# Two prompt tiles of a decoder step share the weight units of their first feed-forward input, and the second tile's x loads behind the first unit

## The reference, cut to what matters

```python
def swiglu_ffn(x, w_in, w_out):
    g, u = jnp.split(x @ w_in, 2, axis=-1)
    return (jax.nn.silu(g) * u) @ w_out
...
    x = x + 0.5 * swiglu_ffn(rmsnorm(x, norm_gains[layer, 0]), ffn_w_in[layer, 0], ffn_w_out[layer, 0])
    h = rmsnorm(x, norm_gains[layer, 1])
    ... GLA in layer 0, windowed attention on shared K/V in layer 1 ...
    x = x + y
    x = x + 0.5 * swiglu_ffn(rmsnorm(x, norm_gains[layer, 2]), ffn_w_in[layer, 1], ffn_w_out[layer, 1])
```

## Time and profile before

| | us |
|---|---|
| median of three runs | 2317.02 |
| lowest and highest | 2314.41, 2321.76 |
| the profiled execution | 2332.64 |
| its span on the slowest core (core 1), first to last instruction | 2331.1 |
| span of its fastest core (core 7) | 2302.8 |
| median span of cores 0 to 3, of cores 4 to 7 | 2321.7, 2309.2 |
| PE busy on core 1 | 2290.8 (98%) |

### The profile page before, as it was taken

How to read it: one execution, slowest core, us unless ns; L and a number is a source line. 1 busy time by engine, 2 the same in 40 slices (tenths; PEclk the granted TensorE clock), 3 DMA queues, 4 the chain that set the end, 5 groups by cost and what they waited for, 6 DMA issues and landing times.

```text
span 2331.1 us, 40261 instructions; the slowest of 8 cores (2302.8 to 2331.1 us)
## 1 busy us (share of the span) xinstructions
PE 2290.8 (98%) x13759; PEld 1080.0 (46%) x13759; DVE 1209.4 (52%) x2094; ACT 1142.2 (49%) x2131; POOL 319.6 (14%) x599
## 2 busy tenths in 40 slices
PE   7999999999999989999999999999999999999999
PEld 3444544544444444445444445445444444444444
DVE  4435664566435566357533445645664355735742
ACT  4434745554543465444552256456455335644551
POOL 2111111111111111110111111111111111011110
PEclk9899999999999999999999999999999999999999
DMA  9998898878988999797999899888899999598793
GB/s 176 149 172 151 153 169 139 136 128 156 164 150 139 182 157 171 137 155 148 167 168 174 151 172 155 146 143 146 155 162 166 159 159 164 102 157 145 148 173 87
DMA packets 101464, 357.08 MB, mean 153 GB/s; under 512 B 12400, under 2 KB 17552, under 8 KB 101136
## 3 DMA queue, kind: packets, MB, share of 16 engines
q0 software_dynamic: 84144, 326.25, 84.5%
q1 hardware_dynamic: 16832, 27.21, 3.7%
q10 hardware_dynamic: 288, 1.05, 0.2%
HBM read 663.17 MB, written 15.40 MB: 291 GB/s over the span
## 4 chain that ended last, share of the span: by engine, by line
PE 95%; DMA 2%; issue 1%; ACT 1%; DVE 1%; POOL 0%; DVEq 0%; SPq 0%; ACTq 0%; POOLq 0%
PE pst L634 91%; PE pst L844 1%; DMA ring<-wfo 1%; DMA ring<-wfi 1%; DMA ring<-ck 1%; PE pst L1461 1%; DMA x<-xp 0%; PE pst L1483 0%; PE pst L1523 0%; PE pst L1096 0%; PE pst L1097 0%; PE pst L1079 0%; ACT h L639 0%; DVE h L650 0%; ACT pb L639 0%
## 5 line engine op out<-in xcount | busy, mean ns | idle before, releaser
L634 PE MATMUL pst<-h,ring 128*128 128x512 bf16 x6144 | 1390.7, 383 | 11.0 <-DMA ring<-wfi 4.3
L634 PEld LDWEIGHTS pst<-h,ring 128*128 128x128 bf16 x6144 | 595.9, 98 | 734.1 <-issue 81.9
L634 PE MATMUL pst<-r,ring 128*128 128x512 bf16 x3136 | 713.0, 382 | 0.8 <-DVE x L650 0.8
L639 ACT ACTIVATE pb<-pb 128x512 f32<-128x512 f32 x856 | 534.7, 630 | 74.8 <-DVE pb L928 13.8
L639 ACT ACTIVATE pb<-pst 128x512 f32<-128x512 f32 (+1 forms) x472 | 278.3, 596 | 506.9 <-PE pst L634 496.5
L647 DVE TENSOR_TENSOR pb<-pb,pst 128x512 f32<-128x512 f32 x368 | 251.7, 686 | 487.2 <-ACT pb L639 484.5
L634 PEld LDWEIGHTS pst<-r,ring 128*128 128x128 bf16 x3136 | 303.8, 98 | 363.1 <-issue 30.0
L530 POOL DMA_DIRECT2D ring<-wfi x336 | 177.8, 531 | 1066.6 <-PE pst L634 852.4
L639 ACT ACTIVATE h<-x 128x512 bf16<-128x512 f32 x188 | 116.8, 627 | 366.4 <-DVE x L650 274.5
L647 DVE TENSOR_TENSOR r<-pb,pst 128x512 bf16<-128x512 f32 x336 | 230.0, 687 | 47.0 <-DVE pb L647 40.1
L650 DVE SCALAR_TENSOR_TENSOR x<-pst,x 128x512 f32<-128x512 f32 x128 | 88.2, 689 | 196.0 <-PE pst L634 193.9
(11 more groups left out here) (159 smaller groups left out, 1006.2 us busy)
## 6 DMA issues: line engine op xcount, KB each, us to landing
ring<-wfi POOLq DMA_DIRECT2D x336, 512.0 KB, 9.5
ring<-wfo POOLq DMA_DIRECT2D x128, 672.0 KB, 8.6
ring<-wgl POOLq DMA_DIRECT2D x64, 512.0 KB, 10.4
y_p<-x SPq DMA_DIRECT2D x32, 256.0 KB, 6.6
x<-xp SPq DMA_DIRECT2D x14, 512.0 KB, 7.8
ring<-wqd POOLq DMA_DIRECT2D x12, 512.0 KB, 12.8
ring<-wod POOLq DMA_DIRECT2D x16, 384.0 KB, 9.4
ring<-wkv POOLq DMA_DIRECT2D x8, 512.0 KB, 7.6
```

The costliest lines, as they stand in the source:

```text
L634: ins = e.matmul(out, lhsT=l, rhs=r, start=(start and i == 0), stop=(stop and i == last), skip_group_check=skip)
L639: return O(ACT, lambda e: e.activation(out=out, in_=in_, func=func, scale=scale, bias=bias), reads, writes, c_act(n))
```

## The change

For t1's first feed-forward input no units are made: `units[(1, "fi0", j)]` is t0's unit. t1 thus reads `ring0`, and those 21 units have three users (t0, ts, t1). The loads of `ring1` begin with t1's `fo0` units, the first four of which wait for t0's `fi0` units 8, 10, 12 and 14. t1's x quarters wait for units 0, 0, 1 and 1 instead of 3, 5, 7 and 9; in the order of building, unit 3 comes behind all four of them. t1 has rank -15 (ahead of the other prompt tile) until its first norm has been applied, and `LEAD` is 21 units instead of 24. Lines behind L463 lie 3 to 7 further down in the changed file (L634 is L641, L844 is L851).

```diff
--- before.py
+++ after.py
@@ -460,7 +460,10 @@
         def ffn_units(f):
             for j in range(NF):
-                add_unit("fi%d" % f, j, wfi[f * NF + j], 2048)
+                if (t, f) == (1, 0):
+                    units[(1, "fi0", j)] = units[(0, "fi0", j)]
+                else:
+                    add_unit("fi%d" % f, j, wfi[f * NF + j], 2048, 0 if t + f else 3)
             for m in range(8):
                 add_unit("fo%d" % f, m, wfo[f * 8 + m], 2688)
                 if (t, f) == (3, 3) and m % 2 == 0:
@@ -491,13 +494,13 @@
-    LEAD = 24 * 2048
+    LEAD = 21 * 2048
     NWS = 8
     first = {(0, "fi0", 0): [("x", "b0", 3)], (0, "fi0", 1): [("x", "b0", 7)]}
     for k in range(4):
-        first[(1, "fi0", k)] = [units[(0, "fi0", 12 + 2 * k)].key]
+        first[(1, "fo0", k)] = [units[(0, "fi0", (8, 10, 12, 14)[k])].key]
     for t in (2, 3):
         for k in range(1, 6):
             first[(t, "fi0", k)] = [("x", "b%d" % (t % 2), 7)]
@@ -517,6 +520,8 @@
             live = [x for x in live if x not in over] + [(lo, hi, u)] + [(a, lo, o) for a, b, o in over if a < lo] \
                 + [(hi, b, o) for a, b, o in over if b > hi]
             u.ap = ring[:, lo:hi]
+            if u.uid == (0, "fi0", 3):
+                yield need(lambda: ("x", "b1", 7) in S.lastw)
             if u.uid in first:
                 yield need(lambda: all(k in S.lastw for k in first[u.uid]) and (u.uid[0] < 2 or ("xl", u.uid[0]) in done))
             dst = u.ap
@@ -562,6 +567,8 @@
         T.nm, T.i, T.t, T.n = "t%d" % t, i, t, 512
         T.rank = (lambda i=i: 10 if i else 0 if prog[0] - prog[1] <= LEAD else 20)
         T.u, T.slot = t, i
+        if t == 1:
+            T.rank = lambda: 10 if ("h", "t1", 1, 7) in done else -15
         T.b = "b%d" % i
         T.x, T.h, T.pool = xb[i], hb[i], Share(pool, i)
         T.R = rb[i]
@@ -668,7 +675,7 @@
             if T.n == 32:
                 yield need(lambda: "CF" in S.lastw)
             if T.t == 1:
-                after = units[(0, "fi0", 3 + 2 * q)]
+                after = units[(0, "fi0", (0, 0, 1, 1)[q])]
                 yield need(lambda: after.ready)
             w = len(ms) * T.n
             src = xp[T.t] if T.n == 512 else xs
```

## The result

The changed kernel is **slower by 0.6%**: 2334.62 us median of seven runs, against 2317.42 us for the kernel before beside it on the same chip, ratio 1.006 with an interval of 1.0049 to 1.0072 (the medians differ by 17.2 us, the ratio, which leaves disturbed runs out, says 13.9). A second measurement on another occasion gave 1.0064 (1.0049 to 1.0079). The prediction was 2313 us, "same" the likeliest; the measured time is also outside its range (2300 to 2327). The start went as rival C said; to that came a base of comparison that was too high, and a second loss behind the start.

The account below looks back on a forecast made before the run. PE was taken as the bound, through its idle time and slow matmuls. 2 us gained at the start, 2 at t0's attention and 0 elsewhere took the median from 2317.0 to 2313 us; 8-in-10 range 2300 to 2327.

Parts of the forecast that it names:

- rival C: At the start, x comes late: PE stands at t1's ones matmul until 42.6 us, 10 us; 2319 us, chance 0.12.
- What bounds the kernel: Whole program: only PE's idle time (40 us), matmuls slower than 0.2143 us, or fewer matmuls can change the time.
- x's landing: At the start, units 0 to 3 and x together: not before 33.5 us, at the latest 40.3 us.
- the late one: At the start, units 4 and 5 get ahead of x; the ones matmul waits to 42.6 us, 10 us.
- the early case: At the start, x and units 0 to 3 are there at 33.5 us; PE stalls 3.75 us at unit 3.
- The clock behind the stall: Behind PE's early stall, matmuls at a low clock lose 2.0 us.
- rival D: Shared stage: PE without gaps keeps the 0.81 clock for longer; say 2325 us, chance 0.12.
- 2.5 + 0.7 + 1.6 us: Start, core 1: 2.5 + 0.7 lost at 0.81 around 30 to 40 us stay; 1.6 is half the 74-112 us loss.
- The sum for the start: Start, core 1: 3.75 + 0.5 + 2.0 + 3.2 + 1.6 = 11.1 us lost against 13.4, 2.3 us gained.
- Unit 6: After the start, its load, issued near 49 us, lands at 56 to 57, before PE wants it at 57.7; nothing lost.
- t0's attention, 2 us gained: End of t0's attention, where 5.1 us were lost: half counted, 2 us gained, bounds 0 and 5.
- Everything behind, +-5 taken as 0: Elsewhere behind the start, 3.5 us of wfo waits and some ten short ones may come or go: +-5 us, taken as 0.

Follow-up runs that it names:

- a2_x_before_u4: The changed kernel, with the load of weight unit 4 waiting until all of t1's x has landed; ratio 1.0033 to the kernel before.
- d4: The kernel before, with t1's first output matmuls (fo0) held until all of t0's fo0 are issued; ratio 0.9997.
- b1: The kernel before with LEAD 21 instead of 24 units, nothing else changed; ratio 1.0007.

## Why the prediction was wrong

**What bounds the kernel: right.** Only PE's idle time and its low clock set the time. The ledger without what is counted twice leaves the same 2261 to 2265 us in all seventeen profiles.

**x's landing: the step that failed.** "I take the early one" (33.5 us) should have been the late one: 39.6 us, 0.7 us short of the bound of 40.3 that the prediction gave. Rival C's mark, a landing later than 37 us, was passed, and the stalls of 1.99 + 8.58 us on core 0 are C's 10 us. The reason given for the early case was the rows of x's quarters before (7.6 to 12.4 us after issue). These were issued over 25 us; now four quarters were issued within 4.6 us onto five waiting units, and took 10.4 to 18.8 us. I had read a latency as if it didn't depend on what is queued.

The sentence on the Trainium skill, page "DMA: Bandwidth & Descriptors", section "Queues, rings and completion order", pointed the same wrong way by my own arithmetic. The queues of core 0 between 20 and 36 us, weights (q0) and x (q1), as packets, MB and share of the 16 engines:

```profile
q0 software_dynamic: 477, 1.75, 64.7%
q1 hardware_dynamic: 450, 1.65, 35.8%
```

Packets and bytes went about one to one, which fits taking turns between the queues. But I turned "half" into half of the engines' time, at x's own 316 GB/s. A weight packet takes longer: x had 0.36 of the engines' time, and the two queues together moved 3.40 MB in 16 us, 212 GB/s, so 103 GB/s for x: a quarter every 5.1 us. The rule as such is not refuted; its price was. That this sharing is the cause, a2_x_before_u4 shows: with units 4 and 5 kept out of the way x landed at 33.3 us, the early case's 33.5.

**The clock behind the stall: under-sized.** 2.0 us was taken. On core 0, 112 matmuls took 26.70 us after the stall against 24.0 at full clock, 2.7 us. From 60 us on the clock was 1.00: rival D (0.81 for the length of the shared stage) did not occur, nor did the 2.5 + 0.7 + 1.6 us that the sum kept for stretches at 0.81. The ledger has no loss by the clock from 120 to 280 us on any core of the changed kernel, with all eight in dense matmuls. By that, the trace does not bear out the full length of the rule on the Trainium skill's page "TensorE: Matmul & The Clock Gate", section "The HAM clock gate".

**The base of the comparison: mis-sized.** The sum for the start was 11.1 us against 13.4 of the kernel before on core 1. Counted the same way for core 0 after, up to the end of the 51 matmuls at 115.22 us: 315 matmuls x 0.2143 = 67.5, three groups 3.2, small ones 0.4, together 71.1 of 86.1 us, so 15.0 us lost. My sum was 3.9 us too low, by x's late landing. But the 13.4 were core 1 of one execution that lay 15.6 us over the median and had the 0.81 stretches that no other profile has. The prediction had core 7's 6.5 us beside it, and chose core 1's "since the slow die decides". By the same count the kernel before usually loses 8.2 and 8.6 us there (d4 and b1, means of eight cores). The change was credited with 2.3 us; against the usual start it costs 6.4. Even the early case would have gained nothing: a2_x_before_u4, in which x landed as it says, loses 9.0 us by this count, less than the 11.1 of the sum, and still no less than the kernel before.

**Unit 6.** Foretold to be issued near 49 us and to land with 1 us to spare; it was issued at 58.12 us, and still no PE wait followed before 97.76 us (1.10 us), since PE itself was late by as much. The step holds, shifted by the stall. The DMA share of 0.00 for 20 us was not foretold: the saving in bytes lies exactly in a stretch in which nobody asks for bytes.

**t0's attention, 2 us gained: not there.** 820 to 940 us has 11.8 and 13.9 us after, 10.0 to 13.6 in the kernels with own units. PE's wait at t0's last denominators (line 1558) is gone, as foretold, but on every core a wait of 1.0 to 2.5 us stands directly ahead of them, at the values (line 1553).

**Everything behind, +-5 taken as 0: the second failure.** Some waits went, as hoped (400 to 820 us: 1.5 us after, 5.8 before, the waits for `wfo`), others came: 6.9 us at 280 to 400, 8.1 at 1300 to 1420. The net is about 6 us (3 to 8 between single profiles). The bounds nearly held, the value of zero didn't, and I had counted only places at which the old order loses. The last sentence of the prediction, "if waits appear behind 200 us that the timeline of before does not have", came true.

Summed, the forecast was -4 us and the measured ratio says +13.9, 18 us apart: about 4 from x's late landing, 5 from the base, 2 from the attention and 6 from the places behind make 17 of them. Nothing came back for 66 us of DMA time. Rival C had the right mechanism, but its own sum for the start, 11.1 + 6 = 17.1 us, is 2 us above the 15.0 counted: it kept 4.8 us for stretches at 0.81 that didn't come, and was too low elsewhere. Its 2319 lies 12 us under what the ratio gives (2317.0 + 13.9), since it has neither the usual base nor a loss behind the start.

## What to carry to other kernels

Bytes saved in a stretch where the compute engine is the bound buy nothing; what the edit had to do to save them (an earlier load, a tile that must be ready at once) is paid in full. When two queues load at the same time, let the wanted one go alone: a wait on the other queue gave back half of the 0.6% here. And when a hand-tuned interleave is made anew, count where the new order has a norm without other matmuls behind it, and take the base of a comparison from a usual execution, as a mean over cores, rather than from the slowest core of one that lies 15.6 us over the median.
